# A hybrid decoder layer on one core: two sample key loads get buffers of their own, and four pieces of work change places ahead of the first norm

## What is computed

```python
hp = layer_norm(x_prompt, ln_in_g, ln_in_b); hs = layer_norm(x_sample, ln_in_g, ln_in_b)
z = h @ w_in                                   # 1024 -> 2816, in eight parts
qa, ka, va, qb, kb, vb, uc, vc = jnp.split(z, splits, axis=-1)
o_a = moba_attention(...)                      # 6 heads of 64, softmax with ALiBi
o_b = stick_breaking_attention(...)            # 6 heads of 64, sigmoids and a cumulative product
uc = jax.nn.gelu(uc); vc = layer_norm(jax.nn.gelu(vc), lnc_g, lnc_b)
o_c = chunk_spatial_gating(uc, vc, w_s, b_s)   # u * (lower-triangular mix of v + b)
mixed = jnp.concatenate([o_a, o_b, o_c], axis=-1)
h = layer_norm(DEEPNORM_ALPHA * h + mixed @ w_out, ln1_g, ln1_b)
f = jnp.square(jax.nn.relu(h @ w_ff1)) @ w_ff2
h = layer_norm(DEEPNORM_ALPHA * h + f, ln2_g, ln2_b)
```

## Time and profile before

| | us |
|---|---|
| median of 3 runs | 682.44 |
| lowest and highest | 681.54, 683.45 |
| the profiled execution: its time | 685.94 |
| its span in the trace | 684.2 |
| TensorE busy in the span | 668.9 (98%) |
| VectorE, ScalarE, GpSimd busy | 424.2, 321.5, 408.0 |
| mean granted clock of TensorE | 0.988 |

### The profile page before, as it was taken

How to read it: one execution, slowest core, us unless ns; L and a number is a source line. 1 busy time by engine, 2 the same in 40 slices (tenths; PEclk the granted TensorE clock), 3 DMA queues, 4 the chain that set the end, 5 groups by cost and what they waited for, 6 DMA issues and landing times.

```text
span 684.2 us, 14030 instructions
## 1 busy us (share of the span) xinstructions
PE 668.9 (98%) x5499; PEld 642.0 (94%) x5499; DVE 424.2 (62%) x798; ACT 321.5 (47%) x640; POOL 408.0 (60%) x502
## 2 busy tenths in 40 slices
PE   7999999999999899999999999999999999999996
PEld 4999999999998569999999999999999999999995
DVE  7647555576653735578987584774856747636246
ACT  6666656677755514555453533334425234253122
POOL 4554433333443405422898996968959869688417
PEclk9899999999999989999999999999999999999999
DMA  6343321313429843110531321522313115124003
GB/s 229 118 155 126 94 75 50 93 62 93 140 62 343 273 147 124 62 63 1 186 103 55 134 81 62 165 83 70 116 62 125 62 63 185 62 93 155 1 1 131
DMA packets 34006, 73.66 MB, mean 108 GB/s; under 512 B 3988, under 2 KB 19380, under 8 KB 33942
## 3 DMA queue, kind: packets, MB, share of 16 engines
q1 hardware_dynamic: 26822, 68.88, 30.0%
q10 hardware_dynamic: 6864, 3.90, 1.9%
q0 software_dynamic: 256, 0.00, 0.0%
HBM read 67.16 MB, written 5.60 MB: 106 GB/s over the span
## 4 chain that ended last, share of the span: by engine, by line
PE 89%; DVE 3%; DMA 2%; SPq 2%; ACT 1%; issue 1%; POOL 0%; ACTq 0%; DVEq 0%
PE acc L1939 27%; PE acc L2330 21%; PE acc L2300 7%; PE s_bank L2359 3%; PE s_bank L2358 3%; PE s_bank L2357 3%; PE o_bank L2047 2%; PE acc L2359 2%; PE acc L2358 2%; PE acc L2357 2%; PE acc L2318 1%; PE acc L2317 1%; PE acc L2319 1%; PE acc L2033 1%; PE t_bank L2033 1%
## 5 line engine op out<-in xcount | busy, mean ns | idle before, releaser
L745 POOL TENSOR_TENSOR w_lo<-w_raw,w_hi 128x256 fp32r<-128x256 f32 x144 | 121.9, 878 | 160.6 <-ACT w_hi L852 160.6
L825 POOL TENSOR_TENSOR w_lo<-w_raw,w_hi 128x256 fp32r<-128x256 f32 x142 | 119.2, 878 | 31.8 <-ACT w_hi L1226 31.8
L1939 PE MATMUL acc<-h_hi,w_hi 128*128 128x288 f32 (+1 forms) x416 | 130.2, 313 | 2.6 <-DVE h_lo L1320 2.1
L1939 PE MATMUL acc<-h_lo,w_hi 128*128 128x288 f32 (+1 forms) x416 | 120.4, 289 | 0.0
L1939 PE MATMUL acc<-h_hi,w_lo 128*128 128x288 f32 (+1 forms) x416 | 120.3, 289 | 0.0
L1939 PEld LDWEIGHTS acc<-h_hi,w_hi 128*128 128x128 f32 x416 | 79.2, 190 | 5.6 <-DVE h_lo L1320 3.0
L1226 ACT ACTIVATE w_hi<-w_raw 128x512 fp32r<-128x512 f32 x71 | 43.9, 629 | 84.6 <-PE acc L2330 54.5
L1939 PEld LDWEIGHTS acc<-h_lo,w_hi 128*128 128x128 f32 x416 | 79.3, 191 | 0.3
L2330 PE MATMUL acc<-m_hi,w_lo 128*128 128x256 f32 (+1 forms) x384 | 79.2, 287 | 0.0
L2330 PE MATMUL acc<-m_hi,w_hi 128*128 128x256 f32 (+1 forms) x384 | 79.1, 287 | 0.0
L2330 PE MATMUL acc<-m_lo,w_hi 128*128 128x256 f32 (+1 forms) x384 | 79.1, 287 | 0.0
(11 more groups left out here) (396 smaller groups left out, 1855.2 us busy)
## 6 DMA issues: line engine op xcount, KB each, us to landing
w_raw<-weights SPq DMA_DIRECT2D x94, 512.0 KB, 3.5
k_t<-cache_k_a SPq DMA_DIRECT2D x16, 192.0 KB, 3.7
k_t<-cache_k_b SPq DMA_DIRECT2D x16, 192.0 KB, 4.1
v_pg<-cache_v_a SPq DMA_DIRECT2D x8, 192.0 KB, 4.4
v_pg<-cache_v_b SPq DMA_DIRECT2D x8, 192.0 KB, 4.2
k_t<-cache_v_b SPq DMA_DIRECT2D x8, 192.0 KB, 4.5
y_prompt<-y_n SPq DMA_DIRECT2D x6, 256.0 KB, 2.2
xin<-x_prompt SPq DMA_DIRECT2D x4, 256.0 KB, 3.8
```

The lines of the kernel that those rows point to most:

```text
L745: op = pool.tensor_tensor(w_lo[:, slot, part], w_raw[:, stage, part], w_hi[:, slot, part].bitcast(F32), ALU.subtract)
L825: op = pool.tensor_tensor(lo[:, cols], src[:, cols], hi[:, cols].bitcast(F32), ALU.subtract)
L1939: mm = pe.matmul(out, w[:, slot, cols(k)], x[:, ks[k], halves(hf)], start=(fresh and k == 0 and pas == 0), stop=last)
```

## The change

Six edits, with no arithmetic added or removed:

- Keys 14 and 15 no longer use slots 2 and 3 of the ring. `k_t15` lies over `qbd0` and `k_t14` over `dist_r` and part of `sid_r`. Key 14 is issued in the middle of the input units, behind the load of unit 18 and a wait for the last softmax scores of the prompt; key 15 right behind key 13. The semaphores `w2_loaded` are renamed `late_loaded` and serve both.
- VectorE's `normalise(1)` moves from iteration 2 to iteration 1.
- k tiles 0 to 2 of half 1 move ahead of the wait for the gating rows.
- k tiles 0 to 3 of half 2 move ahead of `turn_s_probs(3)`.
- k tiles 0 to 2 of half 4 move ahead of the wait for the last operands.
- ScalarE's `read_out(0)` moves ahead of the stores of the samples' outputs.

```diff
-K_SLOT = (*range(8), 2, 3, 4, 5, 6, 7, 2, 3)
+K_SLOT = (*range(8), 2, 3, 4, 5, 6, 7)
...
         mix.close()
+        late_keys = ExitStack()
+        k_t15 = sb("k_t15", [P, PAGES, PAIRS, PAGE], to=late_keys)
+        after_k = sb("after_k", [P, NB * PAIRS * 32], to=late_keys)
+        k_t14 = sb("k_t14", [P, PAGES, PAIRS, PAGE], to=late_keys)
+        late_keys.close()
...
         def keys_of(n):
 
+            if n >= len(K_SLOT):
+                return (k_t14, k_t15)[n - len(K_SLOT)][:, :]
...
         def keys_sem(n):
 
+            if n >= len(K_SLOT):
+                return late_loaded[n - len(K_SLOT)], 16 * PAGES
...
             for u in range(8, IN_UNITS + 1):
                 load_first(u)
+                if u == 18:
+                    sp.wait_ge(s_ready, 8 * PAIRS)
+                    load_keys(14)
...
-            for n in (12, 13):
+            for n in (12, 13, 15):
                 load_keys(n)
             sp.wait_ge(s_values_done, 1)
             for b4 in range(2):
                 load_values(2, b4)
             sp.wait_ge(s_scores_done, 3)
-            for n in (14, 15):
-                load_keys(n)
...
                 if gi == 4:
+                    read_out(0)
                     act.wait_ge(v_sample, 2)
...
             for q in range(KT + 1):
                 if q in (0, 2, 4, 6):
                     hi_out(W0 + q // 2)
-                read_out(q)
+                if q:
+                    read_out(q)
...
-                if 1 <= n <= 8 * PAIRS:
+                if n == 1 or 3 <= n <= 8 * PAIRS:
                     normalise(n - 1)
...
+                if n == 1:
+                    normalise(1)
                 if n == 1 or i and n < ITEMS and s == 0:
                     stack_q_lo(i, 1)
...
             out_half(0, range(0, 3))
+            pe.wait_ge(kv_new_ready, 2 * PAIRS)
+            out_half(1, range(0, 3))
             pe.wait_ge(m_ready, 2 * PAIRS)
...
             s_values(0)
-            out_half(1, range(0, 4))
+            out_half(1, range(3, 4))
             turn_s_probs(1)
...
-                turn_s_probs(g + 1)
                 if g == 2:
                     pe.wait_ge(mix_steps, 4)
                     out_half(2, range(0, 4))
+                turn_s_probs(g + 1)
+                if g == 2:
                     pe.wait_ge(mix_lo, 1)
                     out_half(0, range(6, KT))
...
             out_half(3, range(4, KT))
+            out_half(4, range(0, 3))
             pe.wait_ge(s_lo_done, 4)
             pe.wait_ge(mix_lo, 2)
             for q in range(4, 2 * KT):
-                done = 0
+                done = 3 if q == 4 else 0
```

More of the change, by code:

```diff
@@ L367, in hybrid_layer @@
         t_summed = sem("t_summed")
-        w2_loaded = [sem(f"w2_loaded{j}") for j in range(STAGE)]
+        late_loaded = [sem(f"late_loaded{j}") for j in range(STAGE)]
         s_summed = sem("s_summed")
@@ L548, in raw_sem @@
             s = (v + 2) % 4
-            return (w_loaded[s], 16 * ((FF0 + 3 * FG) // 2 + v // 4 + 1)) if s < 2 else (w2_loaded[s - 2], 16 * (v // 4 + 1))
+            return (w_loaded[s], 16 * ((FF0 + 3 * FG) // 2 + v // 4 + 1)) if s < 2 else (late_loaded[s - 2], 16 * (PAGES + v // 4 + 1))
         def raw_free(v):
@@ L1068, in _, with read_out @@
             act.activation(v_s[:, 2, :], v_s[:, 1, :], ACT.Sqrt, bias=eps[:, 0:1], scale=1.0 / HD).then_inc(v_sq, 1)
+            def read_out(q):
+                hf, m = OUT_ORDER[q]
+                act.wait_ge(half_done, 2 * IN_UNITS + q + 1)
+                act.activation(res[:, m, halves(hf)], out_bank(q), ACT.Copy).then_inc(acc_act, 1)
             for gi in range(1, 5):
@@ L1107, in hi_out @@
                 act.activation(wo_hi[:, u - IN_UNITS - RING, :], w_raw[:, u % STAGE, :], ACT.Copy).then_inc(hi_done, 1)
[L1109 to L1113, removed]
             def hi_ff(j):
```

## The result

| | before | after |
|---|---|---|
| median of 11 runs each, us | 682.80 | 680.14 |
| lowest and highest | 681.52, 685.60 | 677.45, 682.24 |
| ratio, 95% interval | | 0.9949 (0.9932 to 0.9966) |
| profiled execution, its span | 685.94, 684.2 | 682.24, 680.5 |
| mean granted clock of TensorE | 0.988 | 0.993 |

The change makes the kernel faster by 0.5%, about 3.5 us, where 5.9 us were forecast. The two medians differ by only 2.7 us, the means of the same runs (683.27 and 679.60) by 3.7; the changed kernel's runs lie in two clusters, five up to 678.5 us and six from 680.1 us on, and the median is the lowest of the upper one. As it stands it lies 0.3 us above the high end of the range; counted from the forecast's own 682.44 us, the ratio gives 679.0 us, inside the range.

A forecast was written before the change was run, and what follows sets the result against it. TensorE, busy 668.9 of 684.2 us, was taken as the bound, so only its waits and clock counted. Gains 1.4 + 3.9 + 0.6 = 5.9 us, off the median 682.44, gave 676.5 us; range 674.5 to 679.8.

The forecast's parts named there:

- Part 1: Score item 1's normalisation moves up on VectorE, ending TensorE's wait at 51.77 us; gain 1.4 us, bounds 0.7 and 1.5.
- Part 2: Three k tiles of output half 1 move ahead of the gating wait; gain -0.1 us, bounds +0.5 and -0.3.
- Part 3: Keys 14 and 15 load earlier: 5.1 us of key wait and half clock saved, less a 1.2 us new wait; gain 3.9.
- The new wait: TensorE would wait 1.2 us for the third group's last values page (v_pg); bounds 0 and 2.2.
- Part 4: Output half 2 goes ahead of the third turn of probabilities, covering any wait there; gain 0.
- Part 5: Earlier read-out of half 0 and k tiles of half 4 end the idle at 258.56 us; gain 0.6, bounds 0 and 0.7.
- signs of being right: No wait near 50 us or before half 4, which starts 5.9 us earlier; full clock; v_pg largest wait; s_pt some 0.7.
- sign of being wrong: Any of: clock under 1.00 between 230 and 260 us, values wait over 2 us, new TensorE wait after 262 us.
- A: Rival: the clock falls all the same around the sample scores and values, costing 2.8 us; 679.3 us, chance 0.12.
- B: Rival: slower; the clock falls near 229.7 us and stays at 0.50 through short waits to 250; 686.5 us, chance 0.03.
- C: Rival: gains stay local, lost to VectorE waits and half 7's weights; only the keys' gain remains; 678.5 us, chance 0.12.
- D: Rival: third group's values land as late as the keys did, wait over 2 us, clock falls; 680.4 us, chance 0.07.

The follow-up runs named there:

- e1: Kernel before with only the normalisation of score item 1 moved up on VectorE; 681.77 us, ratio 0.9969.
- e5: Changed kernel run again, unaltered, for a second profile; 679.51 us, ratio 0.9951 to the kernel before.
- e11: Changed kernel run again, unaltered, for a third profile; 679.16 us, ratio 0.9941 to the kernel before.
- e9: Kernel before run again, unaltered, for a second profile; 684.19 us against 682.85 of the same kernel beside it, ratio 1.0015.
- e10: Kernel before run again, unaltered, for a third profile; 683.81 us.
- e8: Changed kernel with half 1's moved k tiles put back and keys 12 and 13 issued ahead of the second group's values; 681.27 us, ratio 0.9965.
- e7: Changed kernel with half 1's moved k tiles put back and two of four bias transfers moved behind the second group's values; 678.58 us, ratio 0.9947.
- e2: Kernel before with only keys 14 and 15 moved as in the change; 681.05 us, ratio 0.9958.
- e4: Changed kernel without the eight small block-weight transfers on GpSimd's queue (sample outputs then not the reference's); 679.45 us, ratio 0.9937.

## Why the prediction was right in direction and too large

**Part 1, 1.4 us: right.** Three profiles of the kernel before take 7.28, 6.74 and 7.25 us from item 3 to 5, the changed kernel 5.97, 5.70 and 5.69. The means differ by 1.3, and e1 gives 2.1 (0.9 to 3.4).

**Part 2, -0.1 us: its steps came as written.** The turns start later against the work in front of them: 2.84 us ahead of before at half 0 and 2.17 at the turns, so 0.7 late of the forecast 0.8. The second group's values then wait for ScalarE's s_pt, 0.46 us, though 0.2 less than the 0.7 named. The wait of 0.49 us for the gating rows is gone in exchange. With the pages taken off, the seven profiles of the second table show 0.1 us or less for this part, as forecast. What I didn't see is that it takes 0.3 us of slack from the second group's last page.

**Part 3, 3.9 us: the term that was mis-sized.** The saving of 5.1 us was 2.3 of wait and 2.8 of half clock, both read from one execution. Against that execution the sum nearly holds: from half 0 to half 10 parts 3 and 5 were to bring 4.5 us, and 60.16 less 56.05 (the mean of e5 and e11) is 4.1. Against the two other profiles of the kernel before, 58.93 in the mean, it is 2.9. The step that failed is in the first section: "worked out in the profiled execution and taken off the median". That execution took 685.94 us, the median run 682.44. Of the 3.5 us between them, the 1.2 us by which its stretch is longer than those of e9 and e10 was counted as gain. It was a rare execution: of the 83 runs of this kernel beside e1, e5 and e9, 6 had a mean clock as low as its 0.988, and the middle one had 0.993. The forecast named the gap and didn't ask what it consisted of.

**The new wait, 1.2 us at v_pg:** it is there in part. The third group's values take 0.9 us more than their 1.45 in e5, 0.1 in e11 and nothing in the first profile. The wait that I left out is that for the second group's last page: 1.41, 0 and 0.81 us of TensorE's own in three profiles. In the one with 1.41 the clock went down behind it, and its stretch is 3.5 us longer than that of the two others (59.57 less 56.05). As a mean over three, that is 1.2.

**Part 4, 0: right.** The turn behind half 2 shows no wait. **Part 5, 0.6: right.** Half 5 starts 3.77 us ahead of before (258.32 against 262.09) where the work behind the third group's values was 3.12 ahead (242.43 against 245.55), so 0.65 us came free; of these, half 7 keeps all but 0.2 (264.72 against 268.27 is 3.55).

**The sum with these sizes:** all three profiles of each kernel taken alike, half 0 to half 10 takes 59.34 us before and 57.22 after. That is 2.1 us, and with the 1.3 of part 1 it makes 3.4 us, against 3.3 to 4.0 measured. From the 5.9 forecast to these 3.4 there are four steps: 0.1 in part 1; 0.4 in parts 3 and 5 where the clock stays up; 0.8 because the first profile of the kernel before is longer than the mean of three; 1.2 for the late page with the fallen clock, in one profile of three. With three profiles each, the last two are rough.

**Signs.** Of the signs of being right, two came: no wait near 50 us, and none ahead of half 4. The others came in part or not: half 4 starts 3.7 us before 258.56 instead of 5.9, s_pt is waited for 0.46 us instead of 0.7, and the largest wait of TensorE in the stretch is for w_raw, not v_pg. And one sign of being wrong came in the first profile: a clock under 1.00 between 230 and 260 us.

**Rivals.** A (the clock falls all the same) happened in one profile of three, but at the second group. Its 679.3 us lie close to the measured 679.0, and that is luck: its price came in one execution of three only, and the rest of the gap came from the size of part 3. B (the clock stays down through a series of short waits) didn't: the slow stretch lasted 6.8 us, as in the first profile of the kernel before. C (the gain stays local) is out, since all of it up to half 10 reaches the end (the last product starts 3.63 us earlier, half 10 did 3.43). D (the third group's values as late as the keys) is out: no wait of TensorE for them in three profiles.

The Trainium skill, TensorE: Matmul & The Clock Gate, section "A second HAM failure mode: psum-queue depth-cycling", which describes a clock that swings between its levels where short idles recur, had been set beside A and B. The runs here show no swinging: one fall at most between 228 and 250 us in each of 14 profiles, and of the ten with the new keys only the first of the changed kernel has one.

## What to carry to other kernels

Before a stall of one profile is taken off the median of the runs, look at how far that profile stands from the median: part of the difference may be in the stalls. Here the mean of three profiles of the unchanged kernel would have cut the forecast from 5.9 to about 5 us; most of the rest was a page that I hadn't followed. When an engine is made to come earlier, check every load that it uses from there on for slack, the nearest first: a page that lands just as it is needed becomes the next wait. And look at the weight loads' waits as well as TensorE's own.

## What the runs showed of the hardware

The length of a wait doesn't decide whether the clock falls. With key waits of 1.46, 1.51, 1.74 and 2.32 us it fell each time, and with 0.46 and 1.41 us close together too, but not with 1.98 us in e8, nor with 0.46 and 0.81 in e11. Nor does the fall wait for TensorE to go on. In the three profiles of the kernel before, the clock fell at 238.0, 237.4 and 237.6 us, 0.2 to 0.6 us before the wait ended; in e1 1.3 us and in the changed kernel 0.6 us after its end (windows of 0.1 us). Ahead of the waits TensorE was at narrow products of the samples, in e8 too. Through the waits it was hardly busy: 0.29 us of 2.00 at 236 to 238, 0.47 of 2.00 at 228 to 230 in e8. What sets e8 apart stays open.

The clock also falls at the start of the kernel, in some executions and not in others. At 18 to 22 us the first profile of the kernel before and the first of the changed one read:

```profile
18.00:20.00 2.00, 2.00 (x9) 1.59 (x10) 1.31 (x4) 1.68 (x3) 1.94 (x3) 0.50 0.11 45
20.00:22.00 2.00, 2.00 (x10) 1.98 (x9) 1.33 (x3) 0.68 (x2) 0.00 (x0) 0.50 0.49 154
```
```profile
18.00:20.00 2.00, 1.76 (x14) 1.32 (x12) 1.32 (x3) 1.50 (x3) 2.00 (x3) 1.00 0.28 113
20.00:22.00 2.00, 2.00 (x15) 1.78 (x14) 1.75 (x5) 1.77 (x5) 0.11 (x1) 1.00 0.42 88
```

Score item 3 starts between 46.52 (e7, a full clock) and 49.33 us (e2, 0.50 from 16 to 22) over the 14 profiles, and no edit touches TensorE's work up to there. Between 14 and 24 us, 3.4 us of clock are lost in nine profiles, 1.7 in two and none in three (the first of the changed kernel, e4 and e7). Of the 3.7 us between the two first spans, 1.5 are there before item 3, and they are no work of the change. It fits the spread of the runs as well: of the 83 runs of the kernel before, the 27 with a mean clock of 0.990 or less take 684.5 us in the mean, the 28 with 0.995 or more 681.7. Which of the two places the clock was lost at isn't known for runs without a profile.
